# TensorE's order in a slot of an attention phase: one head's transposes moved ahead of the first of two decode pieces

## The chip, the core and the metric

The program runs on one core of one Trainium2 chip. The metric is the device time of one execution in microseconds (us); for the kernel before it is the median of three runs.

## What is computed

The reference is one inference step of a two-layer decoder trunk, for one prompt of 1024 rows and for 8 decode samples of 8 new rows each. Layer 0 is a convolution mixer. Layer 1 is attention with 16 heads of 64 features, and with a forget term that adds a bias to each score. What matters here is the attention of layer 1, in fp32:

```python
def fox_attend(q, k, v, cq, ck, q_pos, k_pos):
    s = jnp.einsum('bqhd,bkhd->bhqk', q, k).astype(jnp.float32) * (HEAD_DIM ** -0.5)
    s = s + (jnp.transpose(cq, (0, 2, 1))[..., :, None] - jnp.transpose(ck, (0, 2, 1))[..., None, :])
    s = jnp.where(k_pos[None, :] <= q_pos[:, None], s, jnp.finfo(jnp.float32).min)
    p = jax.nn.softmax(s, axis=-1).astype(v.dtype)
    return jnp.einsum('bhqk,bkhd->bqhd', p, v)
```

The prompt attends to itself, causally. Each decode sample attends to 4096 cached rows and its own new ones. The cache lies in pages of 128 rows in HBM, 512 KB for a page of keys and as much for a page of values; a page table says which. After the attention come a gate, an output projection and an embedding add, for all rows.

## The kernel before, in words

The work runs in phases: the convolution layer, its output projection, projections for keys, queries, values and gates, then the attention phase, then a tail with the last projections. The change touches the attention phase alone. In it two kinds of work are interleaved on every engine by lists that are fixed when the program is built.

**Slots** carry the prompt. There are 128, x = 0 to 127. Slot x belongs to the pair of heads b = x // 16 and to t = x % 16; t // 2 picks a block of 128 queries from `order = (0, 7, 1, 6, 2, 5, 3, 4)`, and t % 2 picks the head of the pair. A block with index i attends to i + 1 blocks of 128 keys, so two neighbouring slots have 1, 1, 8, 8, 2, 2, 7, 7, 3, 3, 6, 6, 4, 4, 5, 5 blocks. One head's way: TensorE makes the scores in PSUM (L873 to L879); VectorE takes the row maximum and negates it (L2008, L2012); ScalarE takes the exponential with its sum (L1309); VectorE divides by the sum (L2020, L2022); in the next slot TensorE transposes the probabilities into PSUM banks 5 and 6 (`prompt_transpose`, L895) and ScalarE copies them out to PT (L1319); for every second head TensorE multiplies PT with the values (`prompt_pv`, L921). From slot 16 on each slot also has one piece of the output projection of the pair before (`out_product`, L910), which writes bank 5 and which VectorE adds to X3 (`out_add`, L2044).

**Ticks** carry decode. Each sample takes 36 ticks. Ticks 0 to 15 make the scores of 8 groups of 4 key pages: an even tick is the first half of a group (L766 for the bias, then eight of L769), the odd one the second half. Ticks 18 to 33 multiply 8 groups of value pages with the transposed probabilities, half a group each (sixteen of L826). Ticks 16, 17, 34 and 35 have none of this. After an odd tick some have side work (`decode_side`): the transposes of the sample's probabilities (L813), the scores of the new rows, or the transposing of a finished sample (L796). `ticks_of[x]` gives slot x two ticks (early even, late odd), one (late) or none. By the program's formula, in slots 1 to 127 an early tick has work on TensorE in 81 slots, of which 70 come after slot 16. VectorE and ScalarE have nothing to do for an early tick: what they do for a group hangs on its second half.

**Waits.** `prompt_transpose(x - 1, i)` waits for the divided probabilities of slot x - 1 (`s_pn`), for ScalarE's copies of the slot before that (`s_ev`), for `out_add` of slot x - 1 (`s_po`), because that one reads bank 5, and for bank 6 also for decode's copies. `out_product` waits for ScalarE's copy of bank 5 (`s_ev`). The first half of a group waits for its pages (`s_kv`), for the copy of the group before out of PSUM (`s_sc`), or for PTD, ScalarE's copy of the decode transposes (`s_dv`); the second half waits for nothing. Its end frees the group's page buffer (`s_dd`): three buffers KV go round, and the SP queue issues the next four page loads (L538) when one comes free. On ScalarE the order in a slot is: copies of PT of slot x - 1, exponential of slot x, then what the late tick needs. On VectorE: maximum of slot x, division of slot x, `out_add`, late tick. The POOL queue loads queries (L1602, L1604) when scores are done, and keys, values, gates and weights of the next pair at a pair's start.

Of the kernel before, what the change touches and what calls it, by code (L numbers as in the profile page):

```python
# [68 lines left out]
def atleast(eng, sem, value):  # L69

    if not isinstance(value, int) or value > 0:
        eng.wait_ge(sem, value)
# [7 lines left out]
def build(nc, xT, pT, wA, wO, wP, wB, wW, cw, est, cst, fcon, bcon, ck, cv, clf, ptab,  # L80
# [12 lines left out]
    with ExitStack() as ctx:  # L93
# [315 lines left out]
        def copied_after(i):  # L409

            b, r = i // T_B, i % T_B
            return 9 * b + (0 if r < 16 else 1 if r == 16 else 2 + (min(r, 31) - 17) // 2)

        def heads_after(i):
            return max(0, (i - 3) // T_B)

        def new_after(i):
            return 9 * min(i // T_B, DB - 1) + (2 if i % T_B > 0 else -7)
# [4 lines left out]
        def evacs(x, c=None):  # L423

            if x < 0:
                return 0
            b, t = x // 16, x % 16
            before = sum(1 + (order[y // 2] >= 4) for y in range(t))
            return 24 * b + before + 1 + ((order[t // 2] >= 4) if c is None else c)
# [190 lines left out]
        def _(pe):  # L620
# [108 lines left out]
            def decode_tick(i):  # L729

                b, r = i // T_B, i % T_B
                if b == DB:
                    return
                if r < 16:
                    decode_scores(b, r // 2, r % 2)
                if 18 <= r < 34:
                    decode_pv(b, (r - 18) // 2, r % 2)

            def decode_side(i, ev):

                b, r = i // T_B, i % T_B
                if r == 3 and b > 0:
                    heads_transpose(b - 1, ev)
                if b == DB:
                    return
                if r == 1:
                    new_scores(b, ev)
                if r == 16:
                    new_transpose(b, ev)
                if r >= 17 and r % 2 and r < 33:  # L750
                    decode_transpose(b, (r - 17) // 2, ev)
# [107 lines left out]
            def scores(b, t):  # L859

                item, hl, par = order[t // 2], t % 2, b % 2
                n = P * (item + 1)
                q = 8 * b + t // 2
                queries = QI[q % 3]
                if t == 0:
                    pe.wait_ge(s_q[par], 64 * (b // 2 + 1))
                if hl == 0:
                    pe.wait_ge(s_qi[q % 3], 64 * (q // 3 + 1))
                atleast(pe, s_p, 16 * b + t - 1)
                for c in range((n + 511) // 512):  # L870
                    a, e = 512 * c, min(n, 512 * c + 512)
                    out = PS[:, 2 * hl + c, :]
                    pe.matmul(out[:, 0:e - a], BCON[0:96, B_SP + P * hl:B_SP + P * hl + P], CP[par][:, a:e],  # L873
                              start=True, stop=False)
                    if e == n:
                        pe.matmul(out[:, n - P - a:n - a], BCON[:, B_ID:B_ID + P], BCON[:, B_MD:B_MD + P],
                                  start=False, stop=False)
                    pe.matmul(out[:, 0:e - a], queries[:, hl, :], KX[par][:, hl, a:e], start=False, stop=False)
                    mm = pe.matmul(out[:, 0:e - a], queries[:, 2 + hl, :], KX[par][:, hl, a:e], start=False, stop=True)  # L879
                mm.then_inc(s_s, 1)  # L880

            def prompt_transpose(x, i):

                nb = order[x % 16 // 2] + 1
                pe.wait_ge(s_pn, x + 1)
                for c in range((nb + 3) // 4):
                    atleast(pe, s_ev, evacs(x - 1, 0 if c == 0 else None))
                    if c == 0:
                        atleast(pe, s_po, x + 1 - 16)
                    else:  # L890
                        pe.wait_ge(s_dv, copied_after(i))
                        atleast(pe, s_os, heads_after(i))
                        pe.wait_ge(s_sc, new_after(i))
                    for k in range(4 * c, min(nb, 4 * c + 4)):
                        mm = pe.transpose(PS[:, 5 + c, P * (k % 4):P * (k % 4) + P],  # L895
                                          PP[x % 2][:, P * k:P * k + P], IDENT)
                    mm.then_inc(s_trp, 1)

            def out_product(b, t):

                half, mo = t % 2, t // 2
                pe.wait_ge(s_ev, evacs(16 * b + t - 1, 0))
                atleast(pe, s_po, 16 * b - 16 + t)
                if t % 8 == 0:
                    pe.wait_ge(s_wo[t // 8], 16 * b)
                if t == 0:
                    pe.wait_ge(s_o, NQ * b - 1)
                if t == 1:
                    pe.wait_ge(s_o, NQ * b)
                pe.matmul(PS[:, 5, :], WOP[:, P * mo:P * mo + P],  # L910
                          OP[1 - b % 2][:, 512 * half:512 * half + 512], start=True, stop=True).then_inc(s_ou, 1)

            def prompt_pv(b, i):

                pe.wait_ge(s_ev, evacs(16 * b + 2 * i + 1))
                atleast(pe, s_o, NQ * b + i)
                if i == 0:
                    pe.wait_ge(s_vp[b % 2], 16 * (b // 2 + 1))
                for k in range(order[i] + 1):
                    for hl in range(2):  # L920
                        mm = pe.matmul(PS[HD * hl:HD * hl + HD, 7, 0:P], VP[b % 2][:, k, HD * hl:HD * hl + HD],  # L921
                                       PT[hl][:, P * k:P * k + P], start=k == 0, stop=k == order[i])
                mm.then_inc(s_pv, 1)
# [5 lines left out]
            for x in range(N_SLOTS):  # L929
                b, t = x // 16, x % 16  # L930
                early, late = ticks_of[x]
                scores(b, t)
                if early is not None:
                    decode_tick(early)
                if x > 0:
                    prompt_transpose(x - 1, i)
                if late is not None:
                    i = late
                    decode_tick(late)
                if t == 0 and b > 0:  # L940
                    prompt_pv(b - 1, NQ - 1)
                if b > 0:
                    out_product(b, t)
                if t >= 2 and t % 2 == 0:
                    prompt_pv(b, t // 2 - 1)
                if late is not None:
                    decode_side(late, evacs(x - 1))
# [1237 lines left out]
```

## Time and profile before

| | |
|---|---|
| three runs | 2555.23, 2558.25, 2560.53 us |
| median | 2558.25 us |
| profiled execution, its own time | 2548.34 us |
| span of the profiled execution, first to last instruction | 2546.5 us |
| mean granted clock of TensorE | 0.954 |
| busy over the span: TensorE, VectorE, ScalarE, POOL | 90%, 55%, 37%, 45% |
| HBM traffic, mean over the span | 182 GB/s |

The attention slots run from about 1686 us to 2382 us of the span. Times in rows count from the span's start, in us. PE is TensorE's matmuls and PEld its weight loads; DVE is VectorE, ACT ScalarE, POOL GpSimd, SPq the queue of SyncE. "PE L895 x6" is six instructions of line 895. Starts are measured; the ends of matmuls are modelled and overlap the next start a little, so durations of groups are best taken from start to start.

### The profile page before, as it was taken

The numbers are of one execution on the slowest core, as the hardware profiler recorded it, in microseconds if no ns is written. First come the engines' busy times: TensorE is split into PE (matmuls) and PEld (weight loads), VectorE is DVE, ScalarE is ACT, GpSimd is POOL, SyncE is SP. The second block draws the span as 40 slices with busy tenths as digits, with TensorE's granted clock in tenths as the row PEclk, the third lists the DMA queues.
The fourth block names the chain that finished last, engine by engine and source line by source line (L and its number), as shares of the span: only waits on it lengthen the run. The fifth ranks groups of instructions, "written<-read, shape, count | busy, mean of one in ns | idle before, by whom it ended". The sixth has DMA issues, their size and how long they took to land.

```text
span 2546.5 us, 44564 instructions
## 1 busy us (share of the span) xinstructions
PE 2284.5 (90%) x15044; PEld 1844.7 (72%) x15044; DVE 1390.6 (55%) x1990; ACT 949.7 (37%) x1622; POOL 1145.8 (45%) x802
## 2 busy tenths in 40 slices
PE   5999999997449998979999899877999999999799
PEld 4999999997249998969888686634454545545399
DVE  4789988899791016566785211023545455454523
ACT  4556655655351013223332121323343443434311
POOL 0798889988563214444445332232232232222211
PEclk7999999999669998989999999988999999999999
DMA  3222222222033121135635788899999999997312
GB/s 110 73 73 67 72 80 64 73 74 70 18 114 123 45 89 53 65 126 163 182 138 182 258 280 295 287 361 365 387 347 349 349 360 363 357 360 277 117 48 81
DMA packets 143702, 464.36 MB, mean 182 GB/s; under 512 B 28001, under 2 KB 36578, under 8 KB 142386
## 3 DMA queue, kind: packets, MB, share of 16 engines
q1 hardware_dynamic: 117954, 384.07, 43.2%
q0 software_dynamic: 22848, 62.56, 7.4%
q10 hardware_dynamic: 2736, 15.60, 1.5%
q8 instruction: 96, 1.57, 0.3%
q14 instruction: 68, 0.56, 0.1%
HBM read 403.58 MB, written 60.65 MB: 182 GB/s over the span
## 4 chain that ended last, share of the span: by engine, by line
PE 53%; POOL 12%; DVE 11%; issue 8%; DMA 8%; ACT 5%; SPq 2%; ACTq 0%; POOLq 0%; DVEq 0%
POOL ACC L1385 7%; PE PS L610 5%; PE PS L608 5%; PE PS L609 5%; PE PS L703 4%; PE PS L826 4%; PE PS L769 4%; PE PS L705 4%; PE PS L704 4%; PE PS L910 4%; DMA KV<-ck 3%; DMA KV<-cv 3%; PE PS L921 2%; PE PS L895 2%; PE PS L616 2%
## 5 line engine op out<-in xcount | busy, mean ns | idle before, releaser
L1358 POOL TENSOR_TENSOR WL<-RAW,WH 128x1024 fp32r<-128x1024 f32 (+1 forms) x113 | 283.6, 2510 | 454.4 <-ACT WH L995 447.9
L1710 DVE SCALAR_TENSOR_TENSOR PS<-UX,CWT,PS 128x1024 f32<-128x1024 f32 (+1 forms) x672 | 466.3, 784 | 0.0
L641 PE MATMUL PS<-HH,WH 128*128 128x384 f32 (+1 forms) x1152 | 378.9, 329 | 20.7 <-DVE HL L1696 20.7
L643 PE MATMUL PS<-HH,WL 128*128 128x384 f32 (+1 forms) x1152 | 377.8, 328 | 0.0
L642 PE MATMUL PS<-HL,WH 128*128 128x384 f32 (+1 forms) x1152 | 377.6, 328 | 0.0
L703 PE MATMUL PS<-GH,WH 128*128 128x384 f32 (+1 forms) x792 | 272.4, 344 | 29.8 <-DVE KC L1820 16.2
L1385 POOL TENSOR_TENSOR ACC<-ACC,PROD 128x1088 f32<-128x1088 f32 x112 | 284.7, 2542 | 31.3 <-ACT PROD L1047 25.1
L705 PE MATMUL PS<-GH,WL 128*128 128x384 f32 (+1 forms) x792 | 263.5, 333 | 0.0
L704 PE MATMUL PS<-GL,WH 128*128 128x384 f32 (+1 forms) x792 | 262.6, 332 | 0.0
L641 PEld LDWEIGHTS PS<-HH,WH 128*128 128x128 f32 x1152 | 217.6, 189 | 24.7 <-issue 13.7
L1602 POOL DMA_DIRECT2D QI<-qX_scr x128 | 77.7, 607 | 326.4 <-PE PS L879 324.9
L1046 ACT ACTIVATE PROD<-UX,CWT 128x1024 f32<-128x1024 f32 x144 | 165.5, 1149 | 147.1 <-POOL ACC L1385 81.4
L642 PEld LDWEIGHTS PS<-HL,WH 128*128 128x128 f32 x1152 | 218.0, 189 | 0.0
L643 PEld LDWEIGHTS PS<-HH,WL 128*128 128x128 f32 x1152 | 217.8, 189 | 0.0
L1319 ACT ACTIVATE PT<-PS 128x512 f32<-128x512 f32 (+2 forms) x192 | 87.2, 489 | 311.7 <-PE PS L895 311.5
L703 PEld LDWEIGHTS PS<-GH,WH 128*128 128x128 f32 x792 | 151.7, 192 | 68.1 <-issue 36.8
L995 ACT ACTIVATE WH<-RAW 128x1024 fp32r<-128x1024 f32 (+1 forms) x113 | 122.8, 1087 | 187.8 <-PE PS L610 154.0
L608 PE MATMUL PS<-MH,WH 128*128 128x384 f32 (+1 forms) x384 | 133.3, 347 | 45.8 <-POOL ML L1415 45.8
L826 PE MATMUL PS<-KV,PTD 128*32 128x256 f32 x2048 | 137.9, 387 | 15.6 <-DMA KV<-cv 13.2
L704 PEld LDWEIGHTS PS<-GL,WH 128*128 128x128 f32 x792 | 151.7, 192 | 0.1
L705 PEld LDWEIGHTS PS<-GH,WL 128*128 128x128 f32 x792 | 151.4, 191 | 0.0
L2020 DVE RECIPROCAL RIP<-SMP 128x1 f32<-128x1 f32 x128 | 21.0, 164 | 235.9 <-ACT PP L1309 235.9
(224 smaller groups left out, 4667.8 us busy)
## 6 DMA issues: line engine op xcount, KB each, us to landing
KV<-ck SPq DMA_DIRECT2D x256, 512.0 KB, 6.7
KV<-cv SPq DMA_DIRECT2D x256, 512.0 KB, 6.4
RAW<-wA SPq DMA_DIRECT2D x48, 512.0 KB, 3.6
RAW<-wP SPq DMA_DIRECT2D x16, 640.0 KB, 3.8
zT_scr<-ZS ACTq DMA_DIRECT2D x16, 544.0 KB, 2.7
Z<-zT_scr SPq DMA_DIRECT2D x16, 544.0 KB, 3.6
RAW<-wB SPq DMA_DIRECT2D x17, 512.0 KB, 3.7
RAW<-wO SPq DMA_DIRECT2D x16, 512.0 KB, 3.6
```

What stands on the lines that cost most here:

```text
L608: pe.matmul(out, WH[s][:, kk], xh[:, k, a:b], start=first and k == 0, stop=False)
L641: pe.matmul(out, WH[w][:, kk], HH[:, k, a:b], start=k == 0, stop=False)
L642: pe.matmul(out, WH[w][:, kk], HL[:, k, a:b], start=False, stop=False)
L643: mm = pe.matmul(out, WL[w][:, kk], HH[:, k, a:b], start=False, stop=k == KD - 1)
L703: pe.matmul(out, WH[w][:, kk], GH[:, k, a:b], start=k == 0, stop=False)
L704: pe.matmul(out, WH[w][:, kk], GL[:, k, a:b], start=False, stop=False)
L705: mm = pe.matmul(out, WL[w][:, kk], GH[:, k, a:b], start=False, stop=k == KD - 1)
L826: mm = pe.matmul(PS[32 * y:32 * y + 32, 4, 0:4 * HD], PTD[j % 2][:, kk, 32 * y:32 * y + 32], KV[ring(g)][:, kk, 4 * HD * y:4 * HD * y + 4 ...
L1046: act.activation(o[:, 0:SEQ], UX[s][:, j:j + SEQ], ACT.Copy, scale=CWT[s][:, j:j + 1])
L1358: pool.tensor_tensor(WL[s][:, 0:n], RAW[s][:, 0:n], WH[s][:, 0:n].bitcast(F32), ALU.subtract).then_inc(s_lo, 1)
L1385: pool.tensor_tensor(ACC[:], ACC[:], PROD[(s * NT + q) % 2][:], ALU.add).then_inc(s_add, 1)
L1710: i = dve.scalar_tensor_tensor(out=o, in0=x, scalar=w[:, j:j + 1], in1=o, op0=ALU.mult, op1=ALU.add)
```

## The change

In TensorE's program the call of `prompt_transpose` moves up by one place. In a slot with two ticks the order was scores, early tick, transposes, late tick; it becomes scores, transposes, early tick, late tick. In a slot with one tick or none nothing is issued in another order. No instruction is added or removed, the other engines' programs and the queues' stay as they are, and the ticks that the transposes' waits name (`i`, the late tick of an earlier slot) are the same.

```diff
@@ -930,10 +930,10 @@
                 b, t = x // 16, x % 16
                 early, late = ticks_of[x]
                 scores(b, t)
+                if x > 0:
+                    prompt_transpose(x - 1, i)
                 if early is not None:
                     decode_tick(early)
-                if x > 0:
-                    prompt_transpose(x - 1, i)
                 if late is not None:
                     i = late
                     decode_tick(late)
```

## Rows read from the trace of the kernel before

**Rows 1.** Busy time by stretch: us, busy (instructions) per engine, clock, DMA share, GB/s.

```profile
1700.00:1800.00 100.00, 75.16 (x701) 40.33 (x697) 33.06 (x85) 37.43 (x92) 23.54 (x42) 0.88 1.02 379
2200.00:2300.00 100.00, 95.94 (x806) 48.75 (x803) 49.96 (x118) 38.64 (x93) 23.22 (x41) 1.00 0.99 362
```

**Rows 2.** Waits from 1720 to 2320: who waited for whom, us in total, times, longest.

```profile
PE PS L766 <- DMA KV<-ck: 13.7, 2, 13.4
PE PS L895 <- DVE X L2044: 7.1, 14, 0.8
PE PS L826 <- DMA KV<-cv: 6.3, 6, 3.0
```

**Rows 3.** Timeline of PE, slot 47: start, length, line, instructions.

```profile
1957.12 0.39 PE L766 MATMUL PS<-CB,BCON 96*128 96x512 bf16 x1
...
1958.44 0.77 PE L895 MATMUL PS<-FCON,PP 128*128 128x128 f32 x5
1959.13 1.06 PE L769 MATMUL PS<-KV,QDA 128*32 128x512 f32 x8
1960.13 1.13 PE L910 MATMUL PS<-OP,WOP 128*128 128x512 f32 x2
```

**Rows 4.** Timeline of PE before the first slot: two ticks with nothing between them.

```profile
1676.86 0.38 PE L766 MATMUL PS<-CB,BCON 96*128 96x512 bf16 x1 [0.87 <-DMA KV<-ck]
1677.16 1.92 PE L769 MATMUL PS<-KV,QDA 128*32 128x512 f32 x16
1679.02 0.20 PE L781 MATMUL PS<-CB,BCON 96*128 96x64 bf16 x1
```

**Rows 5.** Timeline of PE, transposes before a second half (slot 27), a first half (slot 44).

```profile
1850.04 0.88 PE L895 MATMUL PS<-FCON,PP 128*128 128x128 f32 x6
1850.85 1.07 PE L769 MATMUL PS<-KV,QDA 128*32 128x512 f32 x8
...
1942.26 0.84 PE L895 MATMUL PS<-FCON,PP 128*128 128x128 f32 x6 [0.38 <-DVE X L2044]
1942.94 0.38 PE L766 MATMUL PS<-CB,BCON 96*128 96x512 bf16 x1
```

**Rows 6.** Timeline of PE, value ticks: slot 38 (one tick), slot 54 (two ticks).

```profile
1909.96 0.34 PE L879 MATMUL PS<-KX,QI 128*128 128x384 f32 x1
1910.14 0.38 PE L895 MATMUL PS<-FCON,PP 128*128 128x128 f32 x2
1910.45 1.07 PE L826 MATMUL PS<-KV,PTD 128*32 128x256 f32 x16
...
1993.40 0.33 PE L879 MATMUL PS<-KX,QI 128*128 128x384 f32 x1
1993.66 1.07 PE L826 MATMUL PS<-KV,PTD 128*32 128x256 f32 x16
1994.66 0.44 PE L895 MATMUL PS<-FCON,PP 128*128 128x128 f32 x2
1995.03 1.07 PE L826 MATMUL PS<-KV,PTD 128*32 128x256 f32 x16
```

**Rows 7.** Timeline, slot 40: transposes that come late in a two-tick slot.

```profile
1920.18 0.96 PE L895 MATMUL PS<-FCON,PP 128*128 128x128 f32 x7 [0.84 <-DVE X L2044]
```

**Rows 8.** Timeline, slots 83 and 84: the negated maximum, the exponential, scores' end, the add.

```profile
2147.80 0.15 DVE L2012 TENSOR_SCALAR NMX<-MXP 128x1 f32<-128x1 f32 x1
...
2149.32 1.12 ACT L1309 ACTIVATE PP<-PS,NMX 128x1024 f32<-128x1024 f32 x1
...
2151.15 0.39 PE L766 MATMUL PS<-CB,BCON 96*128 96x512 bf16 x1
...
2151.52 0.67 DVE L2044 TENSOR_TENSOR X<-PS,X 128x512 f32<-128x512 f32 x1
```

**Rows 9.** DMA: a stretch of 10 us (columns as in rows 1), and 1900 to 2200.

```profile
2030.00:2040.00 10.00, 10.00 (x79) 3.83 (x79) 4.85 (x13) 3.83 (x9) 2.22 (x4) 1.00 0.68 234
...
DMA packets 31695, 107.24 MB, mean 357 GB/s; under 512 B 5281, under 2 KB 5281, under 8 KB 31515
```

## The prediction

> **What bounds the kernel now.** I read first the busy times by stretch, then the waits, the timeline slot by slot, and the DMA by stretch. The change acts on the attention slots only, 1686 to 2382 us. Their first part, to about 1800 us, is held by the page loads: DMA is full at 1.02 and 379 GB/s while PE is busy 75% [rows 1]. From there on it is PE: 96% busy in 2200 to 2300 us, and from 1720 to 2320 us it waits 20.0 us for pages in all, 13.4 of them in one wait of the early part [rows 1, 2]. DMA is close behind at 0.99, so what PE gains must also fit under DMA. The third thing to see is that a busy PE is not one stream. Where one kind of matmul follows another, the starts lie further apart than inside one kind. In slot 47 the early tick takes 1.32 us up to the start of the transposes, and the late one 1.00 us up to the output product [rows 3]. The change alters which kinds are neighbours.
>
> **The change, part by part.** The sum is for the 81 slots whose early tick has work on PE; 11 of them are slots 1 to 16, where page loads set the pace (part e), so 70 count, 35 with score ticks and 35 with value ticks.
>
> (a) *The two score ticks become neighbours.* Apart they take 1.32 + 1.00 = 2.32 us [rows 3]. Two neighbouring ticks, with their sixteen L769, stand once in the trace, at full clock: 1679.02 - 1676.86 = 2.16 us to the next kind [rows 4]. That removes 0.16 us. (b) *The transposes now stand before the first half.* Six transposes before a second half take 1850.85 - 1850.04 = 0.81 us to its start; before a first half, which opens with L766, a 128-column matmul as they are, 1942.94 - 1942.26 = 0.68 [rows 5]: 0.13 less. Scores followed by transposes take the same as scores followed by L766, which I put at nothing. Score slots: -0.29 us each.
>
> (c) *Value ticks.* From the last L879 of seven blocks of scores to the transposes is 0.18 us, to a value tick 0.26; two transposes before a tick take 0.31 us where they follow the scores and 0.37 where they follow a tick [rows 6]. That is -0.08 and -0.06. Two neighbouring value ticks stand nowhere in the trace. From above the price is 0: they may keep the distance of two separate ticks. From below I take a little more than the score pair's, -0.20. I choose -0.15, since both kinds use 32-column tiles and the second half waits for nothing. Value slots: -0.29 each, between -0.14 and -0.34.
>
> The Trainium skill, TensorEngine Tiling (Array Packing), Key Properties, has the rule that "Changing tiling mode (not just tile) drains the TensorE". The order before changes mode twice more per two-tick slot than the order after, the trace agrees for score ticks by the 0.16 us above, and no row shows it for value ticks. By this rule (c) would lie at -0.29, without it at -0.14.
>
> (a) to (c): 70 x 0.29 = 20.3 us less. Bounds: 35 x 0.29 + 35 x 0.14 = 15.1, and 35 x 0.29 + 35 x 0.34 = 22.1.
>
> (d) *The cover that the transposes lose.* The early tick stood between scores and transposes and hid waits for the division (L2022) and for `out_add` (L2044) of the slot before. For each of the 70 slots I set the end of the scores against the ends of those two in the timeline. With 0.15 us from the add's end to the transposes, which is what slot 40 shows, they come late by 13.5 us in all, if nothing before them moves. But it does: on ScalarE the exponential of slot x - 1 stands behind the copies of x - 2, which stood behind the early tick. In slot 83 the negated maximum is ready at 2147.95 and the exponential starts at 2149.32 only; it can start some 1.2 us earlier, and the division with it; the add is then bound by its own product and comes 0.6 us earlier. So slot 84, late by 2152.19 + 0.15 - 2151.31 = 1.03 us by the unmoved rows, is late by 0.4 [rows 8] (the scores end 0.16 after L766's start). Slot by slot this leaves 20 slots with 10.4 us: three behind a slot without tick work and with long heads (19, 40, 103) 4.7; five behind a one-tick slot (51, 67, 82, 72, 88) 2.6; twelve with scores of one to three blocks, too short to hide the add, 3.1. Slots 19 and 40 pay 1.1 us of it already, 0.84 of that slot 40 [rows 7], so the change adds 9.3 us. Bounds: 5 if the add starts sooner than I take, 13.5 if ScalarE gains nothing. That such waits are real is seen where one-tick slots have this order already: 14 waits, 7.1 us, 0.5 each [rows 2].
>
> (e) *What the tick gains by standing later.* Value ticks wait for PTD after short scores, in 12 slots 2.4 us in all, up to 0.35; five transposes take 0.7 us and hide it: -2.4. One-tick slots behind two-tick ones get their division sooner: -0.5, an estimate from slots 28, 44 and 112, between 0 and -1. A late page now holds up two ticks and `out_product` behind them, no longer the transposes, copies and exponential; in slots 4 to 16 that fills PE's wait, but the pages come when DMA brings them, so nothing ends sooner. The second half still ends a slot's ticks, so buffers free at the same place, and the SP queue's next loads move only with the sum. POOL's query loads hang on the scores, which lead the slot in both orders. `out_product` waits for ScalarE's copy of bank 5, which now has two ticks as cover, not one; it never was late in these slots, so this is 0.
>
> PE's own sum: -20.3 + 9.3 - 2.4 - 0.5 = -13.9 us, at the bounds -20.5 (-22.1 + 5 - 2.4 - 1.0) and -4.0 (-15.1 + 13.5 - 2.4).
>
> (f) *What DMA takes back.* After 1800 us PE waits for pages at four places (1899, 1906, 2073 and 2239 us), and elsewhere pages land 0.2 to 12 us ahead. Gains made while DMA is full are lost at the next such place; gains made before it has a gap persist, as the loads are released by PE, and gaps there are: 0.68 in 2030 to 2040 us [rows 9]. Slots 34 to 36, 67 to 69 and 97 to 100 lie between a gap and such a place: 0.9 + 0.1 + 1.0. With one more place, where slack is 0.6, I take 3 us back, between 1 and 8.
>
> Profiled execution: 2548.3 - 13.9 + 3 = 2537.4. It lies 9.9 us under the median of the runs shown (2558.25), and I set the same 11 us against that: 2547.
>
> **The rivals.** *DMA holds all of it.* The slots move with the pages, and PE's gain turns into waits for KV at L766 and L826. For it: 0.99 share, slack of 0.1 to 0.7 us at eight groups of pages. Against it: gaps of up to 32% in a 10 us stretch [rows 9], 379 GB/s earlier where 362 are moved here [rows 1], and slack of several us at most groups. It would leave 1 to 3 us of gain: 2556. The Trainium skill, DMA: Bandwidth & Descriptors, Specifications, gives about 358 GB/s as a core's HBM limit; 1900 to 2200 us run at a mean of 357 [rows 9], and by that rule this rival would hold. The 379 GB/s of rows 1 speak against it.
>
> *The chain through VectorE takes the bound (slower).* Place: L895 right behind the scores. If the division comes as late as in the unmoved rows and neighbouring ticks save nothing, the change adds 13.5 - 1.1 = 12.4 us and saves only (b), the first two of (c) and (e): 35 x 0.13 + 35 x 0.14 + 2.4 = 11.9, so PE stands near 0; each two-tick slot must lose 0.1 us more to show. With 0.1 us more latency in each of the 70, 7 us: 2565. It decides once L895's new waits exceed some 23 us. For it: 0.53 us waits in one-tick slots with one block. Against it: rows 4, and ScalarE's idle time before its copies.
>
> *The order does little.* Both gains and waits are half as large, and DMA takes the rest: within 3 us, 2557. That the change doesn't act can't be, with 81 slots reordered.
>
> **How the numbers follow.** Forecast (faster by 5 to 18 us, mostly 11): 0.70, its own range 2541 to 2553. DMA holds it: 0.12. Little: 0.07. Slower: 0.11. I call 0.2% (5.1 us) what a measurement can tell from no change. Faster by more than that: the forecast, and a bit of DMA's case, 0.71. Within: most of the DMA case, the third rival and a piece of the slower one, 0.19. Slower: 0.10. The range 2540 to 2558 holds the forecast, reaches from PE's lower sum with DMA taking 2 (-18.5) to no change, and leaves out the slower side.
>
> **What would show it.** Right: L766 in a two-tick slot reaches the late L769's product in 2.16 us, not 2.32 plus the transposes; two L826 groups need under 2.00 us (1.00 each before); L895 waits for L2044 and L2022 some 16 us (7.1 plus 9.3) in 1720 to 2320 us; L1309 starts right behind L2012; 2200 to 2300 us hold more than 806 matmuls. Wrong: L895 idle over 20 us, waits for KV after 1800 us up by 8 us or more, or a granted clock under 1.00 between 1800 and 2370 us, where it is 1.00 now; I count no clock loss, since PE stays over 90% busy there.

## The result and the profile after

The kernel after takes 2544.65 us (median of 6 runs, 2539.72 to 2547.35), the kernel before 2556.74 in the 6 runs beside and ahead of it (2554.41 to 2560.53). The ratio is 0.995, interval 0.9936 to 0.9963: 12.1 us faster. Forecast were 2547, in 2540 to 2558. The profiled execution took 2539.72 us, its span is 2537.9, 8.6 less than before; before's own profiled execution lay unusually low under its runs, so profile against profile understates the change.

First the busy time by stretch (columns as in [rows 1]), kernel after.

```profile
1890.00:1910.00 20.00, 16.46 (x159) 10.02 (x158) 6.99 (x16) 6.74 (x17) 5.45 (x9) 0.91 1.03 380
...
2030.00:2040.00 10.00, 10.00 (x92) 5.03 (x85) 6.11 (x15) 3.10 (x8) 0.83 (x2) 1.00 0.83 277
...
2200.00:2300.00 100.00, 93.17 (x818) 50.41 (x816) 51.90 (x125) 40.38 (x98) 24.78 (x44) 1.00 1.01 371
...
1800.00:2300.00 500.00, 469.29 (x3992) 252.79 (x3988) 262.49 (x618) 206.52 (x492) 143.79 (x252) 1.00 1.00 363
```

and the last stretch in the kernel before:

```profile
1800.00:2300.00 500.00, 478.19 (x3948) 242.95 (x3947) 256.26 (x606) 199.40 (x482) 139.77 (x245) 1.00 0.99 358
```

The third row answers the second of [rows 1]: 818 matmuls, where 806 stood in the same 100 us, done in 93.17 us of busy time where it was 95.94. The count of so short a stretch says little (the second trace of the kernel before has 816 there, in 96.35 us); over 500 us it is 3992 for 3948 matmuls in 8.9 us less busy time. PE is less busy and yet ahead: what went away was recorded as busy time. The gap in DMA's work that [rows 9] shows in 2030 to 2040 is half closed, 0.83 for 0.68. The first row is the one place that I did not expect: a granted clock of 0.91 inside the slot loop.

Waits in 1720 to 2320 us, kernel after (as [rows 2]).

```profile
PE PS L895 <- DVE X L2044: 13.2, 20, 2.1
PE PS L766 <- DMA KV<-ck: 11.1, 4, 4.9
PE PS L826 <- DMA KV<-cv: 10.9, 5, 3.5
PE PS L910 <- ACT PT L1319: 6.9, 14, 0.7
PE PS L895 <- DVE PP L2022: 1.8, 1, 1.8
```

The transposes wait 15.0 us (13.2 + 1.8), where [rows 2] has 7.1 and one wait of 0.4 for L2022 stood beside it. The 1.8 us are one wait in slot 4, where page loads set the pace. The wait of `out_product` (L910) for the copy is 6.9 us in 14 waits in both kernels.

The timeline of PE, slot 47 and the transposes of 48 (as [rows 3]), and then slot 54 (as [rows 6]), kernel after.

```profile
1956.99 0.73 PE L895 MATMUL PS<-FCON,PP 128*128 128x128 f32 x5
1957.56 0.38 PE L766 MATMUL PS<-CB,BCON 96*128 96x512 bf16 x1
1957.87 1.92 PE L769 MATMUL PS<-KV,QDA 128*32 128x512 f32 x16
1959.73 1.12 PE L910 MATMUL PS<-OP,WOP 128*128 128x512 f32 x2
...
1961.73 0.73 PE L895 MATMUL PS<-FCON,PP 128*128 128x128 f32 x5 [0.53 <-DVE X L2044]
...
1992.77 0.38 PE L895 MATMUL PS<-FCON,PP 128*128 128x128 f32 x2
1993.08 1.93 PE L826 MATMUL PS<-KV,PTD 128*32 128x256 f32 x32
1994.94 1.12 PE L910 MATMUL PS<-OP,WOP 128*128 128x512 f32 x2
```

Slot 47: the two ticks with their L766 take 1959.73 - 1957.56 = 2.17 us. Slot 54: the 32 matmuls of two value ticks take 1994.94 - 1993.08 = 1.86, where they took 1.00 + 1.00 apart. The next slot pays: its transposes wait 0.53 us for the add.

Slots 39 and 40, all engines, kernel after (as [rows 7]).

```profile
1917.51 0.15 DVE L2012 TENSOR_SCALAR NMX<-MXP 128x1 f32<-128x1 f32 x1
1917.70 1.01 ACT L1309 ACTIVATE PP<-PS,NMX 128x896 f32<-128x896 f32 x1 [0.75 <-DVE NMX L2012]
...
1919.63 0.68 DVE L2044 TENSOR_TENSOR X<-PS,X 128x512 f32<-128x512 f32 x1
1920.46 0.95 PE L895 MATMUL PS<-FCON,PP 128*128 128x128 f32 x7 [2.09 <-DVE X L2044]
```

The exponential starts 0.19 us behind the negated maximum (in slot 83 of before it was 1.52, [rows 8]), but slot 40's transposes still wait 2.09 us, because the add ends only at 1920.31.

### The profile page after: what moved, and what is told of

Same layout as the page of the kernel before. It is cut to its first block, busy times and chain, and to the rows that moved or that the text cites. A ratio compares the mean times of both kernels' runs of the same rounds, so it can differ in the third digit from the quotient of the medians.

```text
span 2537.9 us, 44564 instructions
## 1 busy us (share of the span) xinstructions
PE 2269.3 (89%) x15044; PEld 1856.3 (73%) x15044; DVE 1394.9 (55%) x1990; ACT 955.2 (38%) x1622; POOL 1146.9 (45%) x802
## 4 chain that ended last, share of the span: by engine, by line
PE 53%; POOL 12%; DVE 11%; issue 9%; DMA 8%; ACT 5%; SPq 2%; ACTq 0%; POOLq 0%; DVEq 0%
POOL ACC L1385 7%; PE PS L610 5%; PE PS L608 5%; PE PS L609 5%; PE PS L703 4%; PE PS L705 4%; PE PS L704 4%; PE PS L826 4%; PE PS L769 4%; PE PS L910 4%; DMA KV<-ck 3%; DMA KV<-cv 3%; PE PS L921 2%; PE PS L616 2%; PE PS L895 2%
## 5 line engine op out<-in xcount | busy, mean ns | idle before, releaser
L826 PE MATMUL PS<-KV,PTD 128*32 128x256 f32 x2048 | 130.5, 388 | 18.6 <-DMA KV<-cv 18.6
L608 PE MATMUL PS<-XH,WH 128*128 128x384 f32 (+1 forms) x384 | 127.9, 333 | 16.4 <-DVE XL L1804 14.2
```

The source lines that it names most:

```text
L608: pe.matmul(out, WH[s][:, kk], xh[:, k, a:b], start=first and k == 0, stop=False)
L826: mm = pe.matmul(PS[32 * y:32 * y + 32, 4, 0:4 * HD], PTD[j % 2][:, kk, 32 * y:32 * y + 32], KV[ring(g)][:, kk, 4 * HD * y:4 * HD * y + 4 ...
```

## The experiments

Each kernel ran beside the kernel before; the first four shared one chip, the half-page kernels and the repeat of after a second, the rest a third. Below, "slots 17 to 123" is the time from the first matmul of slot 17 to that of slot 124 in the profiled execution, and the "own part" is this less PE's waits for pages and queries. Before: 564.6 us, of it 5.8 of waits for pages and queries, own part 558.8, and in the own part 7.3 us in which PE is idle ahead of the transposes. After: 555.3, waits 8.6, own part 546.7, idle ahead of the transposes 13.9. The diffs leave out lines between, and are against the kernel after where nothing else is said.

**Score slots alone, value slots alone.** The order of after only where the early tick is a score tick (or, second kernel, a value tick):

```diff
+                first = early is not None and early % T_B < 16   # second kernel: >= 16
-                if x > 0:
+                if x > 0 and first:
                     prompt_transpose(x - 1, i)
                 if early is not None:
                     decode_tick(early)
+                if x > 0 and not first:
+                    prompt_transpose(x - 1, i)
```

> The transposes move ahead of the early tick only where that tick makes decode scores (35 two-tick slots after slot 16); where it multiplies values the old order stays. Theory (neighbours of one kind are cheaper, and the lost cover costs what the slot-by-slot tally says): PE saves 35 x 0.29 = 10.2 us and waits 6.9 us more at the transposes (slots 19, 40 and 103 alone 3.6), so -3.3 us for PE and about -2.5 us in time, 0.999 of the kernel before. Each moved slot without a wait is 0.29 us shorter from scores to scores. Rival (the gain comes from the value ticks' later place, PTD and pages, not from neighbours): no moved score slot is shorter, and the time goes up by the waits, +7 us. Rival (all is held by DMA): no change within 1 us.

> The transposes move only where the early tick multiplies values (35 two-tick slots after slot 16). Theory: PE saves 35 x 0.29 = 10.2 us, 2.4 us of waits for PTD, and waits 1.6 us more at the transposes: -11.0 us for PE, of which DMA takes 2 to 4 back, so -7 to -9 us, 0.997 of the kernel before. Rival (two neighbouring value ticks save nothing, since no row of before showed them): 0.14 us a slot, -5.7 us for PE and about -4 in time. Rival (DMA holds it): within 1 us.

Measured: 2549.61 us, ratio 0.9975 (0.9964 to 0.9986), and 2549.26, ratio 0.9979 (0.9966 to 0.9992). The ratios miss 1 by 0.25% and 0.21%, together 0.46%, and the whole change by 0.5%. Neither kind carries it alone. I had put 0.999 for the first, which came out better, and 0.997 for the second, which lies within its interval. The moved slots are shorter as expected, by a median of 0.29 us of either kind. In the single profiles the own part falls from 558.8 to 557.3 and to 553.0 us; both hold pieces at half of TensorE's clock (see the repeat of after below), the value-slot kernel two of 6.8 us and the score-slot kernel one of 3.4. Waits in 1720 to 2320 us, score-slot kernel:

```profile
PE PS L895 <- DVE X L2047: 12.7, 19, 2.1
```

and value-slot kernel:

```profile
PE PS L895 <- DVE X L2047: 7.7, 15, 0.8
```

(the add has moved from L2044 to L2047). The waits that the change adds lie in the score slots, 5.6 us of them; in the value slots 0.6.

**Transposes behind both ticks.** This makes the ticks neighbours too, but on the other side.

```diff
                 scores(b, t)
-                if x > 0:
-                    prompt_transpose(x - 1, i)
                 if early is not None:
                     decode_tick(early)
                 if late is not None:
-                    i = late
                     decode_tick(late)
+                if x > 0:
+                    prompt_transpose(x - 1, i)
+                if late is not None:
+                    i = late
```

> Both ticks stand right behind the scores and the transposes behind both, ahead of the output product: the ticks are neighbours as in the changed kernel, but nothing covers ScalarE's copy of the transposes before the output product. Theory: from the first tick to the end of the second 2.16 us (scores) and 1.87 us (values) as in the changed kernel, and some 0.1 us saved where transposes meet the output product, but 0.4 to 0.75 us of wait for the copy in each of 70 slots; +0.3 us a slot, PE +20 us, time +15 to +20 us (1.007 of before). The waits of L895 for L2044 fall under 7 us. Rival (neighbours save nothing, the cover is all): +38 us. Rival (the copy is hidden or cheap, so the gain is neighbours alone): -10 us or more.

Measured: 2600.46 us, ratio 1.0179 (1.0166 to 1.0192), 45.6 us slower than before, where I had put 15 to 20. That is even more than the 38 us of the rival in which neighbours save nothing, so the time alone can't refute it; the timeline does. The timeline of PE, slot 50:

```profile
1972.62 0.39 PE L766 MATMUL PS<-CB,BCON 96*128 96x512 bf16 x1
1972.94 1.92 PE L769 MATMUL PS<-KV,QDA 128*32 128x512 f32 x16
1974.79 0.77 PE L895 MATMUL PS<-FCON,PP 128*128 128x128 f32 x5
1976.20 1.12 PE L910 MATMUL PS<-OP,WOP 128*128 128x512 f32 x2 [0.64 <-ACT PT L1320]
```

and the waits in 1720 to 2320 us:

```profile
PE PS L910 <- ACT PT L1320: 44.7, 86, 0.9
...
PE PS L895 <- DVE X L2045: 2.8, 5, 0.8
```

The pair still takes 2.17 us (1974.79 - 1972.62), so the ticks' gain is there on either side of the transposes. But ScalarE's copy now has no cover: `out_product` waits 44.7 us for it, 6.9 in after. The waits for the add nearly vanish, 2.8 us. I had forgotten that the 21 slots with one tick are moved as well, median +0.72 us each, 10.4 in all. The 70 with two lose 29.6, more than I had put, since the saving at the handover was smaller than I took: set against the half-page kernel in the old order (below), which has no page waits either, these 70 slots have 37.9 us more idle time and are 33.8 us longer, so they save only 0.06 us each beside the waits. So the late tick has to stand between transposes and `out_product`, and the early one may stand on either side.

**Nine slots keep the old order**, those where the transposes wait longest:

```diff
+                first = x not in (19, 40, 48, 51, 64, 67, 72, 88, 103)
```

(used as `first` above.)

> The changed kernel, but the nine slots whose transposes come late by more than the 0.29 us that they save (19, 40, 48, 51, 64, 67, 72, 88, 103) keep the old order. Theory: the waits are lost cover and belong to the slots where they show, so PE gains the waits less the neighbours' saving, 0.94 x 2 + 0.85 + 0.52 + 0.45 + 2 x 0.24 + 0.17 = 4.4 us more than the changed kernel; slot 19 stands ahead of a place that is held by pages and gives nothing in time, and DMA takes back part of the rest: 2 to 3 us under the changed kernel, so 0.994 of the kernel before, with L895's waits for L2044 and L2022 together down from 15.0 to about 9 us. Rival (DMA takes all that is gained beyond the changed kernel): the same time as it, with the waits for KV up by 3 to 4 us. Rival (the wait moves on to the next slot): L895's waits stay above 12 us and the time does too.

Measured: 2542.78 us (2538.17 to 2544.88), ratio 0.9958 (0.9945 to 0.9971). Waits, this kernel:

```profile
PE PS L826 <- DMA KV<-cv: 10.2, 5, 3.7
...
PE PS L895 <- DVE X L2047: 6.8, 15, 0.9
```

The transposes' waits are gone as planned, 6.8 us for 13.2. Slots 17 to 123 take 554.5 us, 0.8 less than after, own part 544.6. The time can't be told from after's.

**Half pages.** To take DMA out, page loads from group 48 on move 512 of their 1024 columns; the rest of the decode pages' data is stale, so `y_sample` isn't the reference's. The kernel before, the kernel after and the nine-slot kernel have this edit:

```diff
-                    sp.dma_start(KV[s][:, kk, :], at(ck if t < NG else cv, page)).then_inc(s_kv[s], 16)
+                    half = D if g < HALF_FROM else D // 2
+                    sp.dma_start(KV[s][:, kk, 0:half], at(ck if t < NG else cv, page)[:, 0:half]).then_inc(s_kv[s], 16)
```

> The kernel before, with half of the page bytes from page group 48 on (first used near 1800 us): each page load moves 512 of the 1024 columns, the rest of a buffer keeps older pages; same instructions, same waits. It shows what pages cost in the old order. Theory: after 1800 us the waits for KV (4.8 us in the profile of before) and the waits for queries (about 1 us) go, and nothing else changes on PE; the profile falls by 5 to 6 us, the median by as much or somewhat more, as other executions may wait more for pages. Rival (the attention slots are bound by DMA): the time falls by tens of us.

> The changed kernel with the same halved page loads from group 48 on, to be set against the kernel before with halved loads. Theory: without page waits PE's own sum shows: 13.9 us less than the old order with half pages (70 slots at -0.29, +9.3 of waits at the transposes, -2.4 for PTD, -0.5), all of it after slot 17, where the full-page profiles show -9.3. The difference of the two is what DMA takes back, 4 to 5 us. Rival (the pages take nothing; the tally of PE is too high): the difference stays at 9 to 10 us. Rival (part of the gain is that transposes run while a late page is waited for): the difference falls below 9 us.

> The version in which nine slots keep the old order, with the same halved page loads. Theory: 4.4 us under the changed kernel with half pages, since with full pages only part of these 4.4 us came out of the profile and pages took the rest. Rival (the nine waits do not cost what they show, since the slots behind them wait less): 1 to 2 us as with full pages.

Measured: 2547.52, ratio 0.9959 (0.9945 to 0.9972); 2532.44, 0.9905 (0.9889 to 0.992); 2530.44, 0.9895 (0.988 to 0.991). Busy time by stretch, old order:

```profile
1800.00:2300.00 500.00, 482.39 (x3983) 244.98 (x3983) 258.77 (x616) 200.81 (x487) 144.27 (x252) 1.00 0.66 208
```

and new order:

```profile
1800.00:2300.00 500.00, 476.53 (x4069) 256.91 (x4068) 267.43 (x630) 211.47 (x505) 148.78 (x261) 1.00 0.67 211
```

DMA is at 0.66 and 0.67, and no slot from 17 to 123 waits for a page. In the same 500 us the new order does 86 more matmuls in 5.86 us less busy time. Slots 17 to 123 take 558.6 and 545.2 us: **PE alone gives 13.5 us**, and the medians lie 15.1 apart. Of the 13.5 the value slots bring 10.3, the one-tick slots 1.4 and the score slots only 1.8: in those the longer waits eat most of what the neighbours save. The full-page pair lies 12.1 apart in its first runs, 14.3 in the later ones (2557.11 to the repeat's 2542.81). So by the medians DMA takes back 1 to 3 us, which their intervals, some 3.5 us to either side, can't tell from nothing. By the slots of the profiled executions it is more: the full-page pair saves 9.3 us there (564.6 - 555.3) and the pair of repeats 7.5 (565.3 - 557.8), so 4.2 and 6.0 are taken back, where I had put 4 to 5, and 2.8 and 2.7 of them as longer waits for pages and queries, the rest in the own part. Pages cost 9.6 us in the old order by the medians (2557.11 - 2547.52), where I had put 5 to 6 for the profile, and 5.9 in its slots; in the new order they cost 10.4 by the medians. The nine-slot kernel gains 2.0 us in the median and 3.4 in its slots, where I had put 4.4.

**The kernel after once more**, unaltered, and the kernel before once more.

> The changed kernel once more, unaltered, beside the kernel before and for a second trace of it. Theory: 0.995 to 0.996 of the kernel before; the slots without a page wait have the same length to 0.02 us as in the first trace, and what differs between the two traces are the waits for KV (22.0 us in the first, from 1720 to 2320 us), by several us. Rival (the slots themselves vary): differences spread over all slots.

> The kernel before once more, for a second trace of it. Its profiled execution (2548.3 us) was shorter than any of its timed ones since (2550.4 to 2564.4). Theory: slots without a page wait are the same to 0.02 us, and this trace has more waits for pages than the 4.8 us after 1800 us of the first, by 3 to 8 us; the median's distance to the first profile is that. Rival: the extra time lies outside the attention slots.

Measured: 2542.81 us, ratio 0.9947 (0.9934 to 0.9961), and one execution of 2552.99. In the repeat of after 95 of the 107 slots are as long as in the first trace to 0.04 us. The own part is 548.5 us, 3.3 above the half-page kernel's 545.2 with the same order. The clock says why. The repeat of after:

```profile
2230.00:2240.00 10.00, 7.40 (x56) 3.70 (x49) 2.79 (x8) 2.14 (x5) 1.70 (x2) 0.83 1.03 374
```

and kernel after, 1898 to 1903 us, with the wait that stands there:

```profile
1898.00:1903.00 5.00, 3.31 (x33) 1.74 (x34) 0.00 (x0) 0.00 (x0) 0.00 (x0) 0.66 1.03 412
...
1899.69 3.23 PE L826 MATMUL PS<-KV,PTD 128*32 128x256 f32 x32 [3.51 <-DMA KV<-cv]
1902.85 0.70 PE L910 MATMUL PS<-OP,WOP 128*128 128x512 f32 x1
```

The pair of value ticks takes 3.16 us here (1902.85 - 1899.69) and 1.86 in slot 54: most of it runs at 0.5 of the full clock, which is 1.2 GHz. Before has no such piece in 1770 to 2370 us, though it waits 2.95 us at the same page.

For the repeat of before I had expected 3 to 8 us more of waits for pages; in slots 17 to 123 it has 0.7 more (6.5 for 5.8). Its span is 4.6 us longer (2551.1 for 2546.5), of which 0.8 us lie ahead of slot 17, 0.8 in slots 17 to 123 and 3.0 behind them. So the rival, that the extra time lies outside, is right here.

**A matmul between the two ticks.** The half-page kernel with the new order, and in 82 slots one bf16 matmul by the identity between the ticks, 128 columns wide or 32. It adds to a PSUM bank of the decode work, so the decode numbers are off by a constant.

```diff
                     decode_tick(early)
+                    if early % T_B < 34 and early < T_B * DB:
+                        pe.matmul(PS[0:128, 4, 0:P], BCON[:, B_ID:B_ID + 128], BCON[:, B_ID:B_ID + P],
+                                  start=False, stop=False)   # second kernel: 32 columns wide
```

> The changed kernel with half pages, and between the two ticks of each of the 82 slots whose early tick has work stands one more matmul of 128 columns width (bf16 identity times 128 columns, added into the decode accumulator, so the decode numbers are off by a constant). Theory (a piece of another tile width between two ticks costs the array a drain at each side, whatever it computes): a pair of ticks grows by the matmul's 0.06 us and the 0.15 us that the change had removed, so 0.2 us a pair, 16 to 17 us over the kernel without it (2532.4). Rival (the saving came from the transposes' semaphore waits and fp32 weight loads, not from the width): a wait-free bf16 matmul costs its own 0.06 us, 5 us in all, the same as the narrow one.

> The same, but the added matmul is 32 columns wide like the ticks' own (the same 128 streamed columns, into the same bank). Theory: no drain, so a pair grows by 0.06 to 0.1 us only, 5 to 8 us in all, and 8 to 12 us less than with the wide one. Rival (width does not matter): as long as the wide one.

Measured: 2552.94 us, ratio 0.9989 (0.9979 to 0.9999), and 2535.92, ratio 0.9923 (0.9906 to 0.994), against 2532.44 without it: +20.5 and +3.5. The timeline of PE, slot 47, wide:

```profile
1952.98 0.38 PE L768 MATMUL PS<-CB,BCON 96*128 96x512 bf16 x1
1953.29 1.07 PE L771 MATMUL PS<-KV,QDA 128*32 128x512 f32 x8
1954.29 0.23 PE L940 MATMUL PS<-BCON 128*128 128x128 bf16 x1
1954.45 1.06 PE L771 MATMUL PS<-KV,QDA 128*32 128x512 f32 x8
1955.44 1.13 PE L912 MATMUL PS<-OP,WOP 128*128 128x512 f32 x2
```

narrow:

```profile
1955.11 0.38 PE L768 MATMUL PS<-CB,BCON 96*128 96x512 bf16 x1
1955.42 1.07 PE L771 MATMUL PS<-KV,QDA 128*32 128x512 f32 x8
1956.30 0.22 PE L940 MATMUL PS<-BCON 128*32 128x128 bf16 x1
1956.31 1.07 PE L771 MATMUL PS<-KV,QDA 128*32 128x512 f32 x8
1957.31 1.13 PE L912 MATMUL PS<-OP,WOP 128*128 128x512 f32 x2
```

none:

```profile
1954.48 0.38 PE L768 MATMUL PS<-CB,BCON 96*128 96x512 bf16 x1
1954.80 1.92 PE L771 MATMUL PS<-KV,QDA 128*32 128x512 f32 x16
1956.65 1.12 PE L912 MATMUL PS<-OP,WOP 128*128 128x512 f32 x2
```

From L768 to L912 it is 2.46, 2.20 and 2.17 us. The same matmul on the same moving data costs 0.29 us a pair when it is 128 columns wide and 0.03 when it is as wide as the ticks. Over slots 17 to 123 it is the same: 0.30 us is the median in the 35 score slots and in the 35 value slots with the wide one, 0.04 with the narrow one. So it is the change of width between neighbours that costs, not one more matmul. The forecasts had the order right and the distance too small: 16 to 17 us for the wide one, 5 to 8 for the narrow one, and 8 to 12 between the two. The narrow one starts 0.88 us behind the first half, the wide one 1.00 behind it: 0.12 are lost on the way from 32 to 128, and more on the way back. A rival is that the wide matmul's 128 columns of weights take longer to load than 32. The same product, identity by 128 columns, stands in every slot's scores between matmuls of 128 columns, here in the wide kernel:

```profile
1952.15 0.23 PE L875 MATMUL PS<-CP,BCON 96*128 96x128 bf16 x1
1952.22 0.22 PE L878 MATMUL PS<-BCON 128*128 128x128 bf16 x1
1952.25 0.30 PE L880 MATMUL PS<-KX,QI 128*128 128x128 f32 x1
```

The next start follows it by 0.03 us. So weights of that size cost little where the neighbours are as wide; no run changed the size of the weights and nothing else. The Trainium skill, TensorEngine Tiling (Array Packing), Key Properties, says that a change of tiling mode drains the engine; the pair of kernels agrees, 17.0 us in the time.

The narrow kernel's own part, 549.4 us, holds one piece at half the clock, in slot 40 (its timeline, then busy time by stretch):

```profile
1916.18 0.96 PE L897 MATMUL PS<-FCON,PP 128*128 128x128 f32 x7 [2.07 <-DVE X L2049]
...
1910.00:1920.00 10.00, 7.51 (x45) 3.59 (x43) 5.87 (x16) 3.62 (x8) 2.82 (x5) 0.87 0.46 135
```

It stands behind the transposes' wait for the add, not behind a wait for a page, and slot 40 is 1.7 us longer than in the kernel without the matmul. After has the same wait in slot 40 (2.09 us) and keeps its full clock.

**Value products ahead of `out_product`** in 19 two-tick slots of the nine-slot kernel, so that L921, 64 columns wide, follows the ticks and the output product follows it (diff against the nine-slot kernel):

```diff
+                values = t in (2, 6, 10, 12, 14) and early is not None and early % T_B < 34
+                if values:
+                    prompt_pv(b, t // 2 - 1)
                 if b > 0:
                     out_product(b, t)
-                if t >= 2 and t % 2 == 0:
+                if t >= 2 and t % 2 == 0 and not values:
                     prompt_pv(b, t // 2 - 1)
```

> The version with nine slots in the old order, and in 19 two-tick slots after slot 16 (t = 2, 6, 10, 12, 14) the product with the values (64 columns wide) stands ahead of the output product (128 columns). Theory (a width change less per slot): the product before a value product takes 1.06 us to the next start and before transposes or scores 0.96, so 0.09 us in each of the 19, 1.8 us in all, of which the measurement sees nothing; 2541 to 2543, the profile's slots show it as -0.09 each. Rival (the add of the output product, now later, exposes the next slot's transposes): +0.3 us and more in the odd slots behind them with 3 blocks or fewer of scores, none of which was chosen, so none.

Measured: 2540.29 us (2535.23 to 2548.37), ratio 0.994 (0.9923 to 0.9957). Slot 22's PE timeline:

```profile
1832.80 0.66 PE L921 MATMUL PS<-PT,VP 128*64 128x128 f32 x8
1833.39 1.12 PE L910 MATMUL PS<-OP,WOP 128*128 128x512 f32 x2
1834.35 0.38 PE L873 MATMUL PS<-CP,BCON 96*128 96x512 bf16 x1
```

It takes 1.55 us from L921 to the next slot's scores, and 1.65 from L910 in the nine-slot kernel. The 19 slots are shorter by 0.09 to 0.16 us, 2.5 in all, where I had put 1.8. The own part is 541.6 us against 544.6; the two traces differ in their pieces at half the clock as well, so this difference is not the order's alone. This is the lowest median of the kernels that compute everything, but its interval overlaps that of after.

## Why the prediction was right

The direction, the mechanism and the size were right, and the time was 2.4 us too high. That it came so near is in part luck, since errors of up to 2.6 us in PE's sum cancel. By its own steps:

**(a) and (b)**: the score pair takes 2.17 us, as forecast from [rows 4], and the slots shorten by the median 0.29 us that the sum has. The two single-kind kernels put the changes of order at 0.25% and 0.21%. In (b), five transposes take 0.57 us to L766 in slot 47 (1957.56 - 1956.99), where they took 0.69 to L769 in [rows 3]: 0.12 less, for the forecast 0.13.

**(c)**: the pair of value ticks takes 1.86 us, 0.14 less than two separate ones; -0.15 was taken by analogy. The matmul-between kernels show why the analogy held. Counted by width, a two-tick slot of before goes 128, 32, 128, 32, 128 and one of after 128, 32, 128: two changes less, 0.29 us in either kind of slot, whatever term of mine the record puts it down to. The wide matmul brings the two changes back, in slots of both kinds, and costs 0.29 a pair, 0.26 more than the narrow one. That the count is not the whole rule is seen where the transposes stand behind both ticks: two changes less there too, but waits in almost every slot, and only 0.06 us saved beside them.

**The term of 20.3 us was too large by 2.6.** In the half-page pair, where no page disturbs, the handovers bring 17.7 us (13.5 + 8.4 of added waits, less 1.4 and 2.8, which the next two points take away). Slots whose transposes don't wait save 0.29 each, those where they wait mostly 0.11 to 0.15 (0.07 to 0.22 in 12 slots). My sum gave every slot the full 0.29 and then added the wait. I read it so that a group behind a wait also loses the early load of its first weights, which [rows 5] could not show; no run isolated this.

**(d)** 9.3 us was expected, of it for L2044 and L2022 in 1720 to 2320 us 7.1 + 9.3 = 16.4. Measured: 15.0 in that stretch, of which 1.8 lie in slot 4 and not in the 70 slots of the sum, and 8.4 added in the two-tick slots of the half-page pair. The unmoved rows would have given 12.4. So the argument on ScalarE holds as a whole: the exponential follows the negated maximum after 0.19 us. Its groups came out one by one: slots 19, 40 and 103 wait 4.8 us together (1.54 + 2.09 + 1.14) for 4.7, the five behind a one-tick slot 2.6 for 2.6, those with short scores 2.2 for 3.1, slot 84 0.31 for 0.4.

**(e)** PTD -2.8 for -2.4, one-tick slots -1.4 for -0.5 (slot 100 gave -0.62 and wasn't on the list), and `out_product` waits as long as before. The sum of PE was -13.9 and is -13.5, because the errors of the first term (+2.6) and of these (-0.9 for the add, -0.4, -0.9) nearly cancel. That is luck.

**(f)** 3 us taken back, of 1 to 8: it is 1 to 3 by the medians, 4.2 and 6.0 by the slots. What failed here is one of my signs that would prove the prediction wrong: the granted clock was to stay at 1.00 in 1800 to 2370 us, and it did not. Waits for KV rose by 6.1 us after 1770 us (12.7 for 6.6 at L766 and L826), by 3.4 in slots 17 to 123 (8.2 for 4.8), and towards the end of one of them, 3.51 us long, the clock fell to half. The sign isn't a clean one: the second trace of the kernel before has 0.83 in 2360 to 2370 us. I had counted no clock loss because PE is busy over 90% there. The loss is some 1.5 to 1.7 us a piece (546.7 with one, 548.5 with two, against 545.2 with none), and it wasn't in my 3 us. The range held all the same.

**The rivals.** *DMA holds all of it* falls: with half the bytes the change brings 15.1 us, with all of them 12.1 to 14.3. The Trainium skill, DMA: Bandwidth & Descriptors, Specifications, has about 358 GB/s as a core's limit to HBM; 371 GB/s moved in 2200 to 2300 us and 412 in 1898 to 1903, and that rule did not hold the stage. *The chain through VectorE is slower* has its place right (L895) and its price wrong: 15 us, not over 23. *Little* falls with the interval, whose upper end is 0.9963, some 9 us below no change.

**The start.** I set the 11 us against the median shown and not against the profiled execution, which lay 9.9 us under it. The later medians of before bear that out (2554.88 to 2557.11). The profiled execution was forecast at 2537.4 us and took 2539.72.

## What to carry to other kernels

On TensorE count the changes of tile width between neighbouring groups of matmuls, and group what has one width; here two changes less were worth 0.29 us a slot where nothing waited, and it stands in the record as busy time, not as a wait. When work moves ahead of what covered its wait, follow the producers' queues too, since what it waits for has moved as well, and take a smaller saving for a group behind a wait. Cover between two dependent groups (the late tick between transposes and output product) is worth more than the width: moving it cost 46 us.

## What was not expected of the hardware

- In a stage where PE is 94% busy, single waits came with some 3.4 us at half of the full clock, at some places with 6.8 us: in 1770 to 2370 us once in after (3.51 us of wait), three times in its repeat, never in before (2.95 us) or with the transposes behind both ticks. It isn't bound to pages: the narrow kernel had such a piece behind a wait of 2.07 us for the add, with DMA at 0.46, and the repeat of before had one at 2366 us, behind waits for VectorE and ScalarE of at most 1.14 us. I can't say from these runs what decides; the score-slot kernel had one behind a wait of 2.33 us, and after kept its clock behind 2.09 us for the add and 2.89 for a page.
- The narrow bf16 matmul between the ticks was nearly free, 0.03 us, though the record gives it 0.22 us; the wide one, recorded with 0.23, cost 0.29.
- The DMA share of 1.00 over 500 us did not bind: halving the bytes of the late pages (363 to 211 GB/s) gave 10.4 us of 2543.
- One profiled execution can lie 8 to 10 us under the median of the timed runs of the same kernel (2548.34 and 2558.25).
